# The first expert begun inside the mixer's program, and the small product's stores waited for by ScalarE

## The chip, the core and the metric

The kernel runs on one core of one Trainium2 chip. The core has five engines with instruction queues of their own: TensorE (PE, with its weight loads PEld), VectorE (DVE), ScalarE (ACT), GpSimd (POOL) and SyncE (SP), and 16 DMA engines that all of them feed. The metric is the device time of one execution in microseconds, given as the median of several runs.

## What is computed

Two transformer blocks over 2048 tokens of width 1024, in float32. The change lies where the first block's mixer ends and its experts begin; the rest, cut here, is combine, a second block with attention and a state-space scan, and an output projection.

```python
h = h + concat([ret, pool]) @ w_out            # mixer, 16 tiles of 128 tokens
hn = rms_norm(h, norm_moe_w)
top_vals, top_idx = lax.top_k(hn @ router_w + router_b, 4)      # 4 of 32 experts
gu = ragged_dot(xs, w_gu, group_sizes) + b_gu[sorted_e]         # xs: rows by expert
act = (up + 1.0) * (gate * sigmoid(1.702 * gate))
y = ragged_dot(act, w_down, group_sizes) + b_down[sorted_e]
...
h = h + gate * (p @ ple_proj_w)                # p @ ple_proj_w is the "small product"
```

## The kernel before

Each phase is a program of its own for the five engines. A phase ends when every engine has reached a barrier; then the engines clear the phase's semaphores, each its share, meet at a second barrier, and begin the next phase. There is no scheduler: the order on each engine is the order in which the code is written, and semaphores written by hand tie the engines together.

**The mixer's end.** After the last of 16 tiles, TensorE works off the small product (`p @ ple_proj_w`, two banks for each tile), ScalarE copies the banks into one of six places of SBUF (`copy_small`, L530), and SyncE stores them to HBM (`store_small`, L389). A copy for tile t waits until the store of tile t - 6 has landed. Beside it VectorE makes the routing tables: `order` (the experts sorted, those with many rows first, L848) and `n_mid`, and GpSimd scatters token numbers into `tok_list`, by expert. At the end SyncE waits for all stores of the small product (L425), since the experts' weights `w_hi` take over that memory.

**The experts.** One loop over 32 experts in the order of `order`. An expert's weights come in 25 units of 512 KB (L1214, SyncE) through five places of a tile `stage`. ScalarE copies a unit to `w_hi` (L1289, "high"), VectorE subtracts that copy from the staged values and writes the rest in bfloat16 to `w_lo` (L1420, "low"), which frees the place for a later unit. Units 0 to 15 are the gate and up weights in four chunks of four units, 16 to 24 the down weights. A tile of rows is gathered by GpSimd: token numbers from `tok_list` (`ids`, L1244), then an indirect load of those rows of `hn` (L1250). TensorE turns the rows (L1635), ScalarE and VectorE split them (L1300, L1302, L1425), and TensorE multiplies them with the four chunks (L1105, L1106 with `w_hi`, L1108 with `w_lo`) into banks `GU`. Chunk 3 uses the bank of chunk 0 again, so it waits until VectorE has added the bias to chunk 0 (L1444); on VectorE that addition stands behind the low part of unit 16.

ScalarE begins the phase with the issue of the five bias loads of the first expert (L1278, L1283), and VectorE with tables of row starts (`tables`, L1516 to L1543), which all engines wait for after the first tile of rows.

Of the kernel before, what the change touches and what calls it, by code (L numbers as in the profile page):

```python
# [142 lines left out]
def mixer_phase(nc, I, S):  # L143
# [3 lines left out]
    with ExitStack() as ctx:  # L147
# [7 lines left out]
        stage = sb("mixer_stage", [P, 5 * 1024])  # L155
# [109 lines left out]
            dve_chain list_zeroed y_zeroed slots_seen totals_ps  # L265
            p_in ple_in ple_high ple_low pT_ps pT_hi_done pT_lo_done pT_bf_done pp_ps pp_sb""".split() + [f"pp_stored{n}" for n in range(PP_SLOTS)]
# [4 lines left out]
        s["scattered"] = S["scattered"]  # L271
        block = ctx.enter_context(nc.Block())
# [10 lines left out]
        def _(sp):  # L283
# [146 lines left out]
        def _(pool):  # L430
# [32 lines left out]
            with pool.Fori(0, TILES) as t:  # L463
                body(t)
        @block.scalar
# [149 lines left out]
        def _(dve):  # L615
# [211 lines left out]
            n_mid, is_long, upto, place, other = (stage[:, 4096 + n * E:4096 + (n + 1) * E] for n in range(5))  # L827
            sel, picked = (stage[:, 2048 + n * E * E:2048 + (n + 1) * E * E].rearrange("p (i e) -> p i e", e=E) for n in range(2))
# [19 lines left out]
            dve.tensor_copy(S["order"][:, :], other)  # L848
            dve.tensor_copy(S["n_mid"][:, :], n_mid)
# [268 lines left out]
def expert_phase(nc, I, S):  # L1118
# [6 lines left out]
    with ExitStack() as ctx:  # L1125
# [6 lines left out]
        stage = S["stage"]  # L1132
# [3 lines left out]
        ids = sb("ids", [P, 1], I32)  # L1136
# [20 lines left out]
            y_stored y_seen dve_chain pool_chain tables_ready tables_seen table_chain low_free""".split()  # L1157
        s = {n: sem(n) for n in names}
        st_in = [sem(f"st_in{b}") for b in range(STAGES)]
        bg_in = [s[f"bg_in{c}"] for c in range(GU_CHUNKS)]  # L1160
        ctx.enter_context(nc.allow_non_contiguous_dma(reason="a tile's token numbers, a word per partition"))
        s.update({f"st_in{b}": x for b, x in enumerate(st_in)})
        ctx.callback(clear_semaphores, nc, dict(s))

        s.update({n: S["keep"].enter_context(nc.semaphore(n)) for n in ("ids_in", "rows_in")})
# [7 lines left out]
        def experts(eng, first, mid, last):  # L1173
# [14 lines left out]
            eng.wait_ge(s["tables_ready"], 1)  # L1188
            eng.sem_inc(s["tables_seen"], 1)
# [19 lines left out]
        def _(sp):  # L1209
# [24 lines left out]
        def _(pool):  # L1234
            ch = Chain(pool, s["pool_chain"])
            make_identity(pool, ch, ident[:, :], s["ident_ready"])
            pool.wait_ge(S["scattered"], 16 * TOPK * TILES)
            pool.sem_inc(s["ids_seen"], 1)

            def gather(slot, g, n):  # L1240


                for h in range(2):
                    pool.dma_start(ids[h * HALF:(h + 1) * HALF, :],  # L1244
                                   S["tok_list"][bass.ds(slot + h * (n - HALF), HALF)]).then_inc(s["ids_in"], 16)
# [14 lines left out]
            def first(i, g):  # L1260
                gather(slot_of(i, 0), g, P)
# [11 lines left out]
        def _(act):  # L1273
# [137 lines left out]
        def _(dve):  # L1411
# [109 lines left out]
            def tables():  # L1521


                part = lambda n: w_lo[:, GU_CHUNKS + n // 2, n % 2 * 4:n % 2 * 4 + 4, :].bitcast(F32).rearrange("p k (i e) -> p (k i) e", e=E)
                sel, picked = part(0), part(1)
                iota, zero, order, n_mid, sorted_mid, cnt_t, ends_t, cnt, ends = (pre[:, n * E:(n + 1) * E] for n in range(9))
                numbers(iota, zero)
                tc.link(dve.tensor_copy(order, S["order"][:, :]))
                tc.link(dve.tensor_copy(n_mid, S["n_mid"][:, :]))
                tc.link(dve.tensor_tensor(sel, row_of_e(iota), row_of_i(order), ALU.is_equal))  # L1530
                tc.link(dve.tensor_tensor(picked, sel, row_of_e(n_mid), ALU.mult))
                tc.link(dve.tensor_reduce(sorted_mid, picked, AX, ALU.add))
                tc.link(dve.tensor_scalar(sorted_mid[:, 0:1], sorted_mid[:, 0:1], 1.0, None, ALU.max))
                tc.link(dve.tensor_scalar(sorted_mid[:, E - 1:E], sorted_mid[:, E - 1:E], 1.0, None, ALU.max))
                dve.tensor_copy(S["n_mid"][:, :], sorted_mid)
                tc.link(dve.tensor_scalar(cnt_t, sorted_mid, 2.0, None, ALU.add))
                tc.link(dve.tensor_scalar(cnt, sorted_mid, 4.0, None, ALU.add))
                tc.link(dve.tensor_tensor_scan(ends_t, cnt_t, zero, 0.0, ALU.add, ALU.add))
                tc.link(dve.tensor_tensor_scan(ends, cnt, zero, 0.0, ALU.add, ALU.add))
                tc.link(dve.memset(S["starts"][:, 0:1], 0))  # L1540
                tc.link(dve.memset(S["rows64"][:, 0:1], 0))
                tc.link(dve.tensor_copy(S["starts"][:, 1:E + 1], ends_t))
                tc.link(dve.tensor_copy(S["rows64"][:, 1:E + 1], ends))  # L1543
                dve.sem_inc(s["tables_ready"], 1)
# [2121 lines left out]
```

## Time and profile before

| | us |
|---|---|
| median of 3 runs | 5382.48 (5380.03 to 5384.93) |
| the profiled execution | 5380.71 |
| its span, first to last instruction | 5378.6 |
| TensorE busy | 5094.7 |
| VectorE busy | 3268.8 |
| ScalarE busy | 2190.6 |
| GpSimd busy | 628.2 |

Busy time is the union of an engine's instructions. All times in rows are microseconds from the start of the span, unless a row is marked ns. A timeline row gives start, duration, engine, line, operation, tiles and the number of instructions merged, then in brackets how long the engine had been idle and what released it. A row "A <- B: total, times, longest" is a wait of A that B ended. The DMA share is the mean busy share of the 16 DMA engines; values over 1 mean that packets overlapped.

### The profile page before, as it was taken

The numbers are of one execution on the slowest core, as the hardware profiler recorded it, in microseconds if no ns is written. First come the engines' busy times: TensorE is split into PE (matmuls) and PEld (weight loads), VectorE is DVE, ScalarE is ACT, GpSimd is POOL, SyncE is SP. The second block draws the span as 40 slices with busy tenths as digits, with TensorE's granted clock in tenths as the row PEclk, the third lists the DMA queues.
The fourth block names the chain that finished last, engine by engine and source line by source line (L and its number), as shares of the span: only waits on it lengthen the run. The fifth ranks groups of instructions, "written<-read, shape, count | busy, mean of one in ns | idle before, by whom it ended". The sixth has DMA issues, their size and how long they took to land. (4 is left out here: it accounts for less than half of the span.)

```text
span 5378.6 us, 78209 instructions
## 1 busy us (share of the span) xinstructions
PE 5094.7 (95%) x25188; PEld 3499.3 (65%) x25566; DVE 3268.8 (61%) x6237; ACT 2190.6 (41%) x3309; POOL 628.2 (12%) x862
## 2 busy tenths in 40 slices
PE   7999999799999999999999999979998899999698
PEld 4666665466666666666666666646665688887365
DVE  5444445577777777777777777754557544443266
ACT  4222222354544445555555555333332533333244
POOL 0000000100000000000000000011100399100000
PEclk9999999899999999999999999989999999999899
DMA  8777777665655657777777777453332400000533
GB/s 283 236 253 235 247 242 217 198 202 179 188 192 179 201 170 235 233 231 235 238 239 237 241 234 236 153 190 140 130 115 99 126 7 7 7 7 9 192 110 107
DMA packets 437589, 938.21 MB, mean 174 GB/s; under 512 B 61152, under 2 KB 86176, under 8 KB 436640
## 3 DMA queue, kind: packets, MB, share of 16 engines
q1 hardware_dynamic: 374816, 774.40, 44.1%
q10 hardware_dynamic: 35328, 87.57, 5.1%
q0 software_dynamic: 27280, 74.02, 4.3%
q8 instruction: 106, 1.74, 0.1%
q14 instruction: 59, 0.48, 0.0%
HBM read 781.97 MB, written 155.98 MB: 174 GB/s over the span
## 5 line engine op out<-in xcount | busy, mean ns | idle before, releaser
L1420 DVE TENSOR_TENSOR w_lo_gate<-stage,w_hi 128x1024 bf16<-128x1024 f32 (+1 forms) x800 | 929.8, 1179 | 188.9 <-ACT w_hi L1289 132.0
L1289 ACT ACTIVATE w_hi<-stage 128x1024 fp32r<-128x1024 f32 (+1 forms) x800 | 791.4, 1017 | 557.0 <-PE GU L1108 299.3
L1105 PE MATMUL GU<-w_hi,x_hl 128*128 128x512 f32 x2048 | 860.8, 420 | 16.5 <-DVE x_hl L1425 10.5
L1106 PE MATMUL GU<-w_hi,x_hl 128*128 128x512 f32 x2048 | 811.7, 396 | 0.0
L1108 PE MATMUL GU<-w_lo_gate,x_bf 128*128 128x512 bf16 x1920 | 479.8, 380 | 7.7
L1105 PEld LDWEIGHTS GU<-w_hi,x_hl 128*128 128x128 f32 x2048 | 387.0, 189 | 132.3 <-issue 32.9
L1105 PE MATMUL Y<-w_hi,a_hl 128*128 128x512 f32 x1024 | 456.7, 446 | 1.7 <-DVE a_hl L1431 1.7
L1106 PEld LDWEIGHTS GU<-w_hi,x_hl 128*128 128x128 f32 x2048 | 388.0, 189 | 83.0
L1106 PE MATMUL Y<-w_hi,a_hl 128*128 128x512 f32 x1024 | 404.4, 395 | 0.0
L1108 PEld LDWEIGHTS GU<-w_lo_gate,x_bf 128*128 128x128 bf16 x2048 | 174.4, 98 | 254.5 <-issue 88.4
L2915 DVE TENSOR_REDUCE ntop<-SC 128x1 f32<-128x2048 f32 x64 | 146.7, 2292 | 268.0 <-PE SC L3028 268.0
L1295 ACT ACTIVATE acted<-pre 128x256 f32<-128x256 f32 (+1 forms) x304 | 132.0, 434 | 383.2 <-DVE pre L1448 373.9
L1250 POOL DMA_INDIRECT rows<-hn,ids x77 | 79.9, 1038 | 1737.0 <-PE TX L1635 1698.8
L1108 PE MATMUL Y<-w_lo_gate,a_bf 128*128 128x512 bf16 x960 | 273.3, 383 | 4.4
L3053 PE MATMUL O<-w_lo_gate 128*128 128x128 f32 x2048 | 265.0, 275 | 0.2 <-ACT w_lo_gate L2846 0.2
L1444 DVE TENSOR_TENSOR pre<-GU,b_gu 128x512 f32<-128x512 f32 x256 | 175.8, 687 | 130.0 <-PE GU L1108 129.4
L3053 PEld LDWEIGHTS O<-w_lo_gate 128*128 128x128 f32 x2048 | 246.2, 191 | 1.8 <-ACT w_lo_gate L2846 0.5
L902 PE MATMUL TR<-mixer_stage,c_all 128*128 128x512 f32 x512 | 230.6, 601 | 17.1 <-DMA mixer_stage<-w_out_rows 15.4
L2243 PE MATMUL G<-w_lo_gate,hT 128*128 128x512 f32 x512 | 227.2, 598 | 3.7 <-ACT hT L1922 3.7
L1105 PE MATMUL Z<-w_in_hi,x_hi 128*128 128x512 f32 (+1 forms) x512 | 214.8, 420 | 13.7 <-DVE x_lo L2030 11.5
L1105 PEld LDWEIGHTS Y<-w_hi,a_hl 128*128 128x128 f32 x1024 | 193.2, 189 | 53.1 <-DVE a_hl L1431 2.1
L1106 PEld LDWEIGHTS Y<-w_hi,a_hl 128*128 128x128 f32 x1024 | 193.9, 189 | 33.8
(635 smaller groups left out, 9178.4 us busy)
## 6 DMA issues: line engine op xcount, KB each, us to landing
stage<-in_expert_w_gate_up_dram SPq DMA_DIRECT2D x512, 512.0 KB, 5.2
stage<-in_expert_w_down_dram SPq DMA_DIRECT2D x224, 512.0 KB, 5.5
mixer_stage<-w_in_lo SPq DMA_DIRECT2D x150, 512.0 KB
mixer_stage<-in_w_out_dram SPq DMA_DIRECT2D x65, 512.0 KB, 9.3
expert_rows<-zero_y SPq DMA_DIRECT2D x64, 512.0 KB
mixer_stage<-w_out_rows SPq DMA_DIRECT2D x64, 512.0 KB
b_gu<-in_expert_b_gate_up_dram ACTq DMA_DIRECT2D x128, 256.0 KB, 4.8
expert_rows<-acted ACTq DMA_DIRECT2D x64, 512.0 KB, 3.3
```

Of the source, the lines that this page charges most:

```text
L902: mm = pe.matmul(out, catT[:, k, :], rows[:, q, :], start=(part == 0 and pair == 0 and q == 0), stop=(part == 1 and pair == 1 and q == 1))
L1105: pe.matmul(out, high(k), w_high(k), start=(k == first), stop=False)
L1106: pe.matmul(out, low(k), w_high(k), start=False, stop=False)
L1108: mm = pe.matmul(out, short(k), w_low(k), start=False, stop=(k == last))
L1250: pool.indirect_dma_start(rows[:, :], None, S["hn"], bass.IndirectOffsetOnAxis(ap=ids[:, :], axis=0)).then_inc(s["rows_in"], 16)
L1289: act.activation(w_hi[:, c, ks, :], staged, ACT.Copy).then_inc(s["hi_done"], 1)
L1295: act.activation(act_of(c)[0:n], gate[0:n], ACT.Tanh, scale=ALPHA / 2).then_inc(s["tanh_ready"], 1)
L1420: dve.tensor_tensor(w_lo[:, c, ks, :], staged, w_hi[:, c, ks, :], ALU.subtract).then_inc(s["lo_done"], 1)
L1444: ch.link(dve.tensor_tensor(pre[:, :], GU[c][:, :], b_gu[:, cols], ALU.add))
L2243: mm = pe.matmul(G[:, n * BANK:(n + 1) * BANK], hT[:, k, :], w_gate[:, k, n * BANK:(n + 1) * BANK], start=(k == 0), stop=(k == KD - 1))
L2915: dve.tensor_reduce(ntop[:, h % 2:h % 2 + 1], SC[:, :], AX, ALU.min).then_inc(s["max_done"], 1)
L3053: mm = pe.matmul(O[:, h * P:(h + 1) * P], c_rows(kt), probsT[:, j, kt % 4 * P:(kt % 4 + 1) * P], start=(kt == 0), stop=(kt == TILES - 1))
```

## The change

Five loads of weights, the load of the first token numbers and the work on tables go from the experts' program to the end of the mixer's; the wait for the small product's stores goes from SyncE at the mixer's end to ScalarE at the experts' beginning.

```diff
@@ mixer, SyncE
-            for t in range(3, TILES):
+            for t in range(3, 9):
                 store_small(t)
-            for n in range(PP_SLOTS):
-                sp.wait_ge(s[f"pp_stored{n}"], 16 * len(range(n, TILES, PP_SLOTS)))
+            sp.wait_ge(s["order_ready"], 1)
+            e = sp.value_load(S["order"][0:1, bass.ds(0, 1)], min_val=0, max_val=E - 1)
+            for m, (c, k0, k1) in enumerate(UNITS[0:STAGES]):
+                w = I["expert_w_gate_up"][0, bass.ds(e, 1), k0 * P:k1 * P, c * BANK:(c + 1) * BANK].squeeze(0)
+                sp.dma_start(S["stage"][:, m, 0:k1 - k0, :], w.rearrange("(k p) n -> p k n", p=P)).then_inc(S["st_in"][m], 16)
+            for t in range(9, TILES):
+                store_small(t)
@@ mixer, GpSimd
+            pool.wait_ge(s["scattered"], 16 * TOPK * TILES)
+            pool.wait_ge(s["order_ready"], 1)
...
+            for h in range(2):
+                pool.dma_start(S["ids"][h * HALF:(h + 1) * HALF, :],
+                               S["tok_list"][bass.ds(slot + h * HALF, HALF)]).then_inc(S["ids_in"], 16)
@@ mixer, VectorE
-            dve.tensor_copy(S["order"][:, :], other)
-            dve.tensor_copy(S["n_mid"][:, :], n_mid)
+            dve.tensor_copy(S["order"][:, :], other).then_inc(s["order_ready"], 1)
+            sorted_mid = is_long
+            ch.link(dve.tensor_tensor(picked, sel, row_of_e(n_mid), ALU.mult))
+            ch.link(dve.tensor_reduce(sorted_mid, picked, AX, ALU.add))
...
@@ experts, all engines
             first(0, 0)
-            eng.wait_ge(s["tables_ready"], 1)
-            eng.sem_inc(s["tables_seen"], 1)
@@ experts, SyncE
-            for m in range(N_UNITS):
-                if m >= STAGES:
-                    sp.wait_ge(s["lo_done"], m - STAGES + 1)
+            for m in range(STAGES, N_UNITS):
+                sp.wait_ge(s["lo_done"], m - STAGES + 1)
                 load(m, e)
@@ experts, ScalarE
-            for c in range(GU_CHUNKS):
+            for n in range(PP_SLOTS):
+                act.wait_ge(s[f"pp_stored{n}"], 16 * len(range(n, TILES, PP_SLOTS)))
+            for m in range(4):
+                high(0, m)
+            bias(0, 0)
+            x_high(0)
+            for c in range(1, GU_CHUNKS):
+                high(0, c + 3)
                 bias(0, c)
+            high(0, 7)
             bias_down(0)
-            for m in range(STAGES):
-                high(0, m)
-            x_high(0)
-            for m in range(STAGES, 16):
+            for m in range(8, 16):
                 high(0, m)
@@ experts, VectorE
-            tables()
-            for m in range(STAGES):
+            for m in range(4):
                 low(0, m)
             x_low(0)
-            for m in range(STAGES, 14):
+            for m in range(4, 14):
                 low(0, m)
```

For this `stage`, its semaphores and `ids` are made before the mixer and live through the whole kernel. The mixer's own staging tile lies on `stage`, and so do tiles of attention (`probs`, `cos`, `sin`), of the scan's output (`toep`, `yT`) and of the last projection (`x2`, `gain_post`, `y_in`, `a_in`), which had memory of their own; VectorE's first tables lie on `c_all` and `vgu`.

SyncE at the end of the mixer, before: `pp` is the small product in HBM, `w_in_room` its place in SBUF, and the branch at L147 is the way to the barrier.

```order
L389 DMA pp<-w_in_room 256x1x512 [waits pp_sb] x13
L147 UNCONDITIONAL_BRANCH [waits pp_stored5,pp_stored4,h_stored,pp_stored3,hn_stored,pp_stored2,y_zeroed,pp_stored1,pp_stored0]
L70 UNCONDITIONAL_BRANCH [waits barrier_Pool_Activation_PE_DVE_SP_release]
L73 ISA x19
L69 UNCONDITIONAL_BRANCH
L1208 UNCONDITIONAL_BRANCH [waits barrier_Pool_Activation_PE_DVE_SP_release]
L1171 TENSOR_LOAD order
L1171 ISA x2
L1214 ISA
L1214 DMA stage<-in_expert_w_gate_up_dram 128x2x512
```

The same place on SyncE, with the change:

```order
L390 DMA pp<-w_in_room 256x1x512 [waits pp_sb] x6
L425 TENSOR_LOAD order [waits order_ready]
L425 ISA x2
L428 ISA
L428 DMA stage<-in_expert_w_gate_up_dram 128x2x512
...
L428 DMA stage<-in_expert_w_gate_up_dram 128x2x512
L390 DMA pp<-w_in_room 256x1x512 [waits pp_sb] x7
L147 UNCONDITIONAL_BRANCH [waits y_zeroed,hn_stored,h_stored]
```

The five loads now stand between the sixth and the seventh of those thirteen stores, and the barrier is reached without a wait for the stores.

ScalarE from the beginning of the experts' program, before: `TX` holds the turned rows.

```order
L1283 DMA b_d<-in_expert_b_down_dram 128x1024
L1289 ACTIVATE w_hi<-stage 128x1024 [waits st_in0]
L1289 ACTIVATE w_hi<-stage 128x1024 [waits st_in1]
L1289 ACTIVATE w_hi<-stage 128x1024 [waits st_in2]
L1289 ACTIVATE w_hi<-stage 128x1024 [waits st_in3]
L1289 ACTIVATE w_hi<-stage 128x1024 [waits st_in4]
L1300 ACTIVATE x_hl<-TX 128x8x128 [waits xT_ps]
```

The same place on ScalarE, with the change:

```order
L1311 ACTIVATE w_hi<-stage 128x1024 [waits pp_stored4,pp_stored3,pp_stored5,pp_stored2,st_in0,pp_stored1,pp_stored0]
L1311 ACTIVATE w_hi<-stage 128x1024 [waits st_in1]
L1311 ACTIVATE w_hi<-stage 128x1024 [waits st_in2]
L1311 ACTIVATE w_hi<-stage 128x1024 [waits st_in3]
L1199 TENSOR_LOAD order
L1199 ISA x2
L1300 ISA
L1300 DMA b_gu<-in_expert_b_gate_up_dram 128x512
L1322 ACTIVATE x_hl<-TX 128x8x128 [waits xT_ps]
```

The first copy now carries the wait for the stores, one unit fewer stands ahead of the rows, and the bias loads come after the first four copies, the last four of them behind the rows.

## Rows read from the trace of the kernel before

**Rows 1.** The page's first part: each engine's busy time, share, instructions.

```profile
PE 5094.7 (95%) x25188; PEld 3499.3 (65%) x25566; DVE 3268.8 (61%) x6237; ACT 2190.6 (41%) x3309; POOL 628.2 (12%) x862
```

**Rows 2.** Stretches: from:to, length, busy of PE, PEld, DVE, ACT, POOL; PEclk, DMA, GB/s.

```profile
955.00:965.00 10.00, 9.93 (x44) 6.41 (x45) 2.96 (x5) 4.33 (x8) 1.08 (x1) 1.00 1.01 123
965.00:975.00 10.00, 9.93 (x45) 6.35 (x44) 0.00 (x0) 4.51 (x8) 0.00 (x0) 1.00 0.65 248
975.00:985.00 10.00, 3.56 (x16) 1.85 (x14) 0.00 (x0) 1.92 (x4) 0.00 (x0) 0.78 0.41 156
...
995.00:1005.00 10.00, 0.06 (x1) 0.09 (x2) 5.73 (x5) 4.23 (x4) 1.76 (x1) 0.50 1.04 390
...
1015.00:1025.00 10.00, 9.93 (x45) 6.68 (x45) 5.63 (x5) 5.17 (x5) 1.07 (x2) 1.00 0.97 340
...
1060.00:1200.00 140.00, 136.49 (x656) 89.40 (x664) 103.97 (x169) 65.18 (x96) 9.40 (x14) 1.00 0.54 171
```

**Rows 3.** Timeline of TensorE from the mixer's last product to chunk 3.

```profile
977.95 0.60 PE L1108 MATMUL PJ<-w_in_room 128*128 128x512 bf16 x2
1004.94 1.94 PE L1635 MATMUL TX<-ident,rows 128*128 128x128 f32 x8 [26.39 <-DMA rows<-hn,ids]
1009.30 0.77 PE L1105 MATMUL GU<-w_hi,x_hl 128*128 128x512 f32 x1 [2.42 <-issue]
...
1026.55 1.90 PE L1108 MATMUL GU<-w_lo_gate,x_bf 128*128 128x512 bf16 x7
1032.04 0.76 PE L1105 MATMUL GU<-w_hi,x_hl 128*128 128x512 f32 x1 [3.60 <-DVEq L1450]
```

**Rows 4.** SyncE around the barrier: timeline, its wait, its semaphore at the barrier.

```profile
979.22 0.53 SPq L389 DMA_DIRECT2D pp<-w_in_room  x1
...
986.71 3.22 SPq L1214 DMA_DIRECT2D stage<-in_expert_w_gate_up_dram  x5
...
SPq L425 <- DMA pp<-w_in_room: 2.8, 1, 2.8
...
L69 SPq EVENT_SEMAPHORE  x1: 17/17/17, 985.6 to 985.6; - x1
```

**Rows 5.** Timeline of GpSimd at the beginning of the experts.

```profile
988.26 1.15 POOL L1244 DMA_DIRECT2D ids<-tok_list  x2 [1.89 <-issue]
996.53 1.76 POOL L1250 DMA_INDIRECT rows<-hn,ids  x1 [7.12 <-DMA ids<-tok_list]
...
1011.46 1.80 POOL L1250 DMA_INDIRECT rows<-hn,ids  x1 [2.61 <-DMA ids<-tok_list]
```

**Rows 6.** The gathered rows from 985 to 1300: duration ns (least/median/most), landing.

```profile
L1250 POOL DMA_INDIRECT rows<-hn,ids x11: 1011/1017/1798, 996.5 to 1293.4; - x11
...
DMA to landing us min/median/max: 4.2/4.7/8.3
```

**Rows 7.** Timeline of ScalarE: small product's copy, bias issues, weight copies.

```profile
977.28 0.60 ACT L530 ACTIVATE w_in_room<-PJ 128x512 f32<-128x512 f32 x1 [0.83 <-PE PJ L1108]
...
986.70 3.72 ACTq L1278 DMA_DIRECT2D b_gu<-in_expert_b_gate_up_dram  x4
...
1008.93 4.83 ACT L1289 ACTIVATE w_hi<-stage 128x1024 fp32r<-128x1024 f32 x5
...
1028.39 1.06 ACT L1289 ACTIVATE w_hi<-stage 128x1024 fp32r<-128x1024 f32 x1 [1.94 <-DMA stage<-in_expert_w_down_dram]
```

**Rows 8.** Timeline of VectorE: order, first split, first bias addition.

```profile
957.80 0.18 DVE L848 CAST order<-mixer_stage 128x32 int32<-128x32 f32 x1
...
994.65 1.23 DVE L1420 TENSOR_TENSOR w_lo_gate<-stage,w_hi 128x1024 bf16<-128x1024 f32 x1 [1.65 <-ACT w_hi L1289]
...
1030.62 0.68 DVE L1444 TENSOR_TENSOR pre<-GU,b_gu 128x512 f32<-128x512 f32 x1
```

**Rows 9.** The store of small tile 9: its issue and landing.

```profile
L389 SPq DMA_DIRECT2D pp<-w_in_room x1: 533/533/533, 962.7 to 962.7; - x1
...
DMA to landing us min/median/max: 5.6/5.6/5.6
```

More of the change, by code:

```diff
@@ L464, in _ @@
                 body(t)
+            pool.wait_ge(s["scattered"], 16 * TOPK * TILES)
+            pool.wait_ge(s["order_ready"], 1)
+            pool.sem_inc(s["lists_seen"], 1)
+            e = pool.value_load(S["order"][0:1, bass.ds(0, 1)], min_val=0, max_val=E - 1)
+            slot = nc.s_assert_within(pool.snap(e * CAP), 0, E * CAP - P,
+                                      skip_runtime_bounds_check_because="an expert has CAP places in the list")
+            for h in range(2):
+                pool.dma_start(S["ids"][h * HALF:(h + 1) * HALF, :],
+                               S["tok_list"][bass.ds(slot + h * HALF, HALF)]).then_inc(S["ids_in"], 16)
         @block.scalar
@@ L826, in _ @@
             dve.wait_ge(s["totals_ps"], 1)
-            n_mid, is_long, upto, place, other = (stage[:, 4096 + n * E:4096 + (n + 1) * E] for n in range(5))
-            sel, picked = (stage[:, 2048 + n * E * E:2048 + (n + 1) * E * E].rearrange("p (i e) -> p i e", e=E) for n in range(2))
+            n_mid, is_long, upto, place, other = (c_all[:, n * E:(n + 1) * E] for n in range(5))
+            sel, picked = (vgu[:, n, 0:E * E].rearrange("p (i e) -> p i e", e=E) for n in range(2))
             row_of_e = lambda ap: ap.unsqueeze(1).to_broadcast([P, E, E])
@@ L847, in _ @@
             ch.link(dve.tensor_reduce(other, picked, AX, ALU.add))
-            dve.tensor_copy(S["order"][:, :], other)
-            dve.tensor_copy(S["n_mid"][:, :], n_mid)
+            dve.tensor_copy(S["order"][:, :], other).then_inc(s["order_ready"], 1)
+            sorted_mid = is_long
+            ch.link(dve.tensor_tensor(picked, sel, row_of_e(n_mid), ALU.mult))
+            ch.link(dve.tensor_reduce(sorted_mid, picked, AX, ALU.add))
+            ch.link(dve.tensor_scalar(sorted_mid[:, 0:1], sorted_mid[:, 0:1], 1.0, None, ALU.max))
+            ch.link(dve.tensor_scalar(sorted_mid[:, E - 1:E], sorted_mid[:, E - 1:E], 1.0, None, ALU.max))
+            dve.tensor_copy(S["n_mid"][:, :], sorted_mid)
+            dve.memset(S["starts"][:, 0:1], 0)
+            dve.memset(S["rows64"][:, 0:1], 0)
+            for table, ends, more in (("starts", upto, 2.0), ("rows64", place, 4.0)):
+                ch.link(dve.tensor_scalar(other, sorted_mid, more, None, ALU.add))
+                ch.link(dve.tensor_tensor_scan(ends, other, zero_e[:, :], 0.0, ALU.add, ALU.add))
+                dve.tensor_copy(S[table][:, 1:E + 1], ends)
         @block.tensor
@@ L3604, in two_blocks @@
             "n_long": sb("n_long", [P, 1], I32),
+            "stage": sb("stage", [P, STAGES, KP, BANK], F32),
+            "st_in": [ctx.enter_context(nc.semaphore(f"st_in{b}")) for b in range(STAGES)],
+            "pp_stored": [ctx.enter_context(nc.semaphore(f"pp_stored{n}")) for n in range(PP_SLOTS)],
+            "ids": sb("ids", [P, 1], I32),
+            "ids_in": ctx.enter_context(nc.semaphore("ids_in")),
             "pos_cur": sb("pos_cur", [P, TOPK], I32),
```

76 lines of the change are left out of this document (26 added, 50 removed).

## The prediction

> **What bounds the kernel now.** I read the page's busy times first [rows 1]: TensorE is busy 95% of the span, so only stretches in which it stands still or waits can give time back. The table of stretches finds the place [rows 2]. In the experts' loop TensorE works 136.49 of 140 us (1060 to 1200). Between the last small product of the mixer, at 977.95, and the first weight product of the first expert, at 1009.30, it only turns one tile of rows [rows 3], and between 995 and 1005 its granted clock is 0.50, the lower of its two levels (1.2 of 2.4 GHz). That hole is 31 us, and a smaller one follows: chunk 2 is issued out about 1028.5, and chunk 3 starts at 1032.04 after 3.6 us of waiting for VectorE [rows 3].
>
> The waits say what ends the hole. SyncE issues the last store of the small product at 979.22 and waits 2.8 us until it has landed; the barrier behind the clearing of semaphores opens at 985.6 [rows 4]. GpSimd then issues the load of the token numbers at 988.26 and stands 7.1 us until they are in, starts the gather of rows at 996.53, and that lands 8.3 us later, the slowest of eleven (4.2, 4.7 and 8.3 are least, median and most) [rows 5, 6]. TensorE turns the rows at 1004.94 and its idle time ends on that gather [rows 3]. While the gather was under way the DMA engines were full: share 1.04 and 390 GB/s [rows 2], with ten units of weights and five bias loads. So the chain is stores, barrier, numbers, gather, turn, and the weights are beside it.
>
> **The change, part by part.** All is reckoned against the profiled execution, span 5378.6 and time 5380.71 us; the median of the three runs is 5382.48, 1.77 more, and I take a difference over from one to the other.
>
> 1. The wait for the stores leaves SyncE. Of its 2.8 us I leave 0.3 for the three waits that stay (h, hn, zeroed rows, all issued long before). The barrier then opens at 985.6 - 2.5 = 983.1. The six waits now stand in ScalarE ahead of its first weight copy; behind them are all its copies, and VectorE and TensorE behind those. The last store lands about 982.6 as before (979.75 + 2.8), ahead of the new start, so I cost them at nothing; the cover is the gather, below, and holds until the landing is some 3 us later.
>
> 2. The numbers are loaded in the mixer. GpSimd's gather takes the place of the load at 988.26, 2.6 us after the barrier, with one of two table reads gone: 2.1 us. New start 983.1 + 2.1 = 985.2 instead of 996.53.
>
> 3. The gather's landing. Bounds are 4.2 and 8.3 us [rows 6]. Five units are in the stage by then, so the queue it met at 996 is gone, but from about 986 SyncE loads units 5 to 8 as VectorE frees places, and VectorE works beside it: the first two gathers took GpSimd 1.76 and 1.80 us against a median of 1.02 [rows 5, 6]. I take the middle, 6.4: rows in at 991.6, turned from 991.7, against 1004.94: 13.2 us earlier (2.5 barrier, 8.8 numbers, 1.9 landing). The weights are ready: four copies of 0.97 us from 983.5 (five in 4.83 us [rows 7]) with VectorE's 1.23 us each behind them [rows 8] end at 989.4. From the turn to the first product is 4.36 us [rows 3], the same instructions in the same order: first product at 996.1 instead of 1009.30.
>
> 4. From there to chunk 3. Before, this took 22.7 us (1009.30 to 1032.04). Chunk 3 needs VectorE's first bias addition, at 1030.62, which stands behind the splitting of unit 16, which ScalarE copied at 1028.39 [rows 7, 8]. Before, five units were split and five staged when the product began; now four are split and five staged, so the refill is one unit behind: 0.52 MB at 390 GB/s, 1.3 us. Four bias loads (3 x 0.26 and 0.52 MB, 3.4 us at that rate) come in here, which were issued at 986.70 before [rows 7]. ScalarE issues them between copies, 0.93 us each (four in 3.72), beside a copy of 0.97. They start while the stage is full and DMA has little to do, and in the ten microseconds from 1015 on DMA moved 340 GB/s [rows 2], not all it can. Bounds: 3.6 us less (the wait ahead of chunk 3 gone, TensorE's three chunks back to back) and 4.7 more (unit and biases in full). I take 1.2 more, near the unit alone. Chunk 3 at 996.1 + 23.9 = 1020.0, that is 12.0 us earlier. After it the order is the old one and the loop is bound by TensorE [rows 2], so the 12.0 us are carried to the end.
>
> 5. The table work on VectorE moves into the mixer. There it runs beside the small products, after the copy of the order at 957.80; VectorE did nothing at all from 965 to 985 [rows 2, 8]. At its old place it cost nothing either: VectorE's first split waited 1.65 us for ScalarE [rows 8]. Moved for free, and the barrier pair that it needed goes too.
>
> 6. Five loads ahead of stores 9 to 15 on SyncE. The order is ready at 958.0 [rows 8]. Stores go out every 2.75 us (store 9 at 962.7, store 15 at 979.22 [rows 4, 9]), so store 8 leaves at about 960; the table read and five issues take some 4 us (five issues in 3.22 [rows 4]), and store 9 waits until about 965. Its data stand behind 2.62 MB, 6.7 us at 390 GB/s: landed at 968.3 before (5.6 us after issue [rows 9]), now about 975. ScalarE needs that landing for its copy at 977.28 [rows 7], the only copy whose place was stored after the loads: 2.3 us to spare. Room for the bytes: DMA's share is 0.65 and 0.41 from 965 to 985 [rows 2], 9.4 us free of 20 against 6.7. Cost: nothing.
>
> The Trainium skill speaks against point 6: its page "DMA: Bandwidth & Descriptors", section "Queues, rings and completion order", says that each DMA engine consumes the descriptors of one queue in ring order. By that, stores cannot pass the loads; no row of before shows it, as no such loads stand there.
>
> 7. The other edits move buffers (the stage now lives through the kernel, tiles of attention and output lie on it). Their instructions and waits stay; I cost them at zero, within 1 us either way.
>
> Sum: 5380.71 - 12.0 = 5368.7 for the profiled execution, 5370.5 on the median's scale. With points 3 and 4 at their ends the gain is 6.6 to 19 us.
>
> **The rivals.**
> *The refill takes it back.* Unit 16 is late by the unit and all bias bytes, 4.7 us instead of 1.2: gain 8.5, or 6.6 with the slowest gather. For it: 390 GB/s for ten microseconds [rows 2]. Against it: the loads start 11 us earlier. 5374.0.
>
> *The gather starts after the splits.* In the new order the gather runs beside VectorE's first four splits, which lasted 1.23 us each. If GpSimd cannot write before they end at 989.4 and the rows land a median 4.7 us later, they come at 994.1, 2.5 us after my 991.6: gain 9.5, 5373.0. Against it: the two gathers beside splits took 0.75 us more, not the length of several splits [rows 5, 6].
>
> The Trainium skill, page "SBUF — State Buffer", section "SBUF: two separate sides", states this rule: a VectorE instruction with two inputs in SBUF and GpSimd share a pair of ports that one holds for a whole instruction while the other is blocked. The 1.76 and 1.80 us bear it out only as far as part of one split. By the rule the gain is 9.5 us, by those two rows 12.0.
>
> *It doesn't do what it says.* If unit 16 comes no earlier than 1028.4, only the barrier's 2.5 us are left, 5380.0. From 986.7 to then 12 units, the biases and two gathers are 8.9 MB: DMA would have to fall to 213 GB/s, where rows show 340 and 390 under load [rows 2].
>
> *Slower: the stores crawl behind the loads.* From 955 to 965 DMA moved 123 GB/s at a share of 1.01 [rows 2]. From 961 on, stores 7 to 15 and the loads are 7.3 MB. At 123 GB/s the last store lands at 1020; ScalarE, now holding the wait, copies four units after that (3.9 us), issues a bias (0.9) and makes the two copies of the rows (some 3 with VectorE's part), so the first product is about 8 us behind, 1028 instead of 1009: with the refill 20 us slower, 5402. It decides against the kernel where the last landing is after some 1000, a mean below 187 GB/s. Against it: 248 GB/s from 965 to 975 with stores alone [rows 2], which went at ScalarE's pace.
>
> **How the numbers follow.** A measurement of this kernel tells about 0.2% from no change, here 10.8 us. Forecast, a gain of 9.5 to 15.5 (5367 to 5373): 0.62. More, with chunk 3 straight behind chunk 2: 0.04. Refill 0.15, splits 0.10, no effect 0.05, slower 0.04. The line of 10.8 us cuts the forecast: four fifths of it, 0.50, are above, with 0.04 and 0.02 of the splits' case that is 0.56 for faster; 0.40 for the same; 0.04 for slower. The range takes gains of 6 to 16 us, 5366.5 to 5376.5, and leaves out the last two cases and the edges, under 0.2.
>
> **What would show it.** In the trace of after: the barrier opening near 983 and no wait of SyncE for the last store; the gather starting near 985 and landing 5 to 8 us later; the rows turned near 992, first product near 996, chunk 3 near 1020, and the same distance from there to the end. ScalarE's copy of small tile 15 still near 977. The forecast is wrong if the small products end later than 980, if ScalarE's first copy is after 988, if the gather lands after 994, or if the loop from 1060 on takes other times than before.

## The result, and the profile after

The kernel after takes 5351.26 us (median of six runs, 5342.78 to 5364.98), the kernel before 5382.3 beside it: a ratio of 0.994, with a 95% interval from 0.9928 to 0.9953. The forecast was 5370.5 with a range from 5366.5 to 5376.5. The gain is 31 us where 12 were forecast, and the time lies below the range. The profiled execution of after took 5342.78 us, its span is 5341.0, 37.6 less than that of before.

The hole at the experts' beginning closed much as forecast. Timelines of after, TensorE first (start, duration, engine, line, operation, tiles, number; in brackets the idle time and what ended it), then SyncE, GpSimd, ScalarE and VectorE:

```profile
986.62 1.94 PE L1636 MATMUL TX<-ident,rows 128*128 128x128 f32 x8 [10.69 <-DMA rows<-hn,ids]
990.98 0.77 PE L1132 MATMUL GU<-w_hi,x_hl 128*128 128x512 f32 x1 [2.42 <-issue]
1007.75 0.58 PE L1132 MATMUL GU<-w_hi,x_hl 128*128 128x512 f32 x1 [4.12 <-DVE w_lo_gate L1447]
1016.39 0.47 PE L1132 MATMUL GU<-w_hi,x_hl 128*128 128x512 f32 x1 [1.38 <-DVEq L1477]
...
959.44 3.01 SPq L428 DMA_DIRECT2D stage<-in_expert_w_gate_up_dram  x5
...
964.96 1.15 POOL L478 DMA_DIRECT2D ids<-tok_list  x2 [11.49 <-issue]
...
982.00 1.05 POOL L1272 DMA_INDIRECT rows<-hn,ids  x1 [1.20 <-issue]
...
974.65 0.60 ACT L546 ACTIVATE w_in_room<-PJ 128x512 f32<-128x512 f32 x1 [0.83 <-PE PJ L1135]
...
982.10 2.00 ACT L1311 ACTIVATE w_hi<-stage 128x1024 fp32r<-128x1024 f32 x2 [5.54 <-DMA pp<-w_in_room]
...
983.19 4.63 DVE L1447 TENSOR_TENSOR w_lo_gate<-stage,w_hi 128x1024 bf16<-128x1024 f32 x4 [23.71 <-ACT w_hi L1311]
```

The gathered rows of after from 980 to 1300, to be set beside [rows 6] (duration in ns, then landing in us, least, median and most):

```profile
L1272 POOL DMA_INDIRECT rows<-hn,ids x11: 1011/1014/1261, 982.0 to 1276.9; - x11
...
DMA to landing us min/median/max: 4.2/4.5/8.9
```

The rows are turned at 986.62 instead of 1004.94 and the first product comes at 990.98 instead of 1009.30 [rows 3]. The numbers are loaded at 964.96 in the mixer, the gather starts at 982.00 instead of 996.53 [rows 5], and ScalarE's first weight copy now waits until the last store has landed (`<-DMA pp`). Chunk 2 has a new wait of 4.12 us, chunk 3's fell from 3.60 to 1.38.

But that is not where most of the gain is. The experts' loop from the first mid tile's first product to the first turned rows of the phase behind it, two rows of before and then the same two of after:

```profile
1055.79 0.52 PE L1657 MATMUL GU<-w_hi,x_hl 128*128 128x512 f32 x1
...
3532.89 0.45 PE L2226 MATMUL TR<-ident,h 128*128 128x128 f32 x1 [29.34 <-DVEq L2044]
```

```profile
1040.86 0.50 PE L1658 MATMUL GU<-w_hi,x_hl 128*128 128x512 f32 x1
...
3498.17 0.45 PE L2227 MATMUL TR<-ident,h 128*128 128x128 f32 x1 [29.28 <-DVEq L2045]
```

After is 14.93 us ahead at the loop's beginning and 34.72 at its end: 2477.10 us became 2457.31 in a stretch whose program the change hardly touches. No wait went away there: from 1080 to 3400 TensorE's longest is 0.9 us in both, and the granted clock from 1100 to 3400 is 1.00, the upper level of 2.4 GHz, in both. From turning to turning, 62 full tiles of 128 rows take 34.31 us each instead of 34.61, one as the other, and the twelve mid tiles of 64 rows 21.95 instead of 22.01 (medians). The gain sits in one kind of product. Groups of TensorE from 2100 to 2900, before and then after (busy time and mean ns of one; the ends are modelled, so a mean holds time that a product waits in the engine, and some bfloat16 records of before are missing):

```profile
L1106 PE MATMUL GU<-w_hi,x_hl 128*128 128x512 f32 x744 | 293.8, 395 | 0.0
L1108 PE MATMUL GU<-w_lo_gate,x_bf 128*128 128x512 bf16 x694 | 173.5, 380 | 2.8
```

```profile
L1133 PE MATMUL GU<-w_hi,x_hl 128*128 128x512 f32 x744 | 290.6, 391 | 0.0
L1135 PE MATMUL GU<-w_lo_gate,x_bf 128*128 128x512 bf16 x743 | 180.5, 381 | 0.0
```

The float32r products are 4 ns shorter, the bfloat16 ones the same. The pitch, from the start of one float32r weight load to the start of the next load, went from 231.8 to 228.4 ns in the mean for the gate and up products, and from 231.4 to 229.8 for the down products.

The rest of the pair's 37.6 us: 2.6 at the mixer's end (its last small product starts at 975.55 instead of 978.18), and 3 behind the loop. In the thirteen traces of this document the mixer ends anywhere from 970.2 to 983.8, with either program, so the 2.6 us can't be put down to the change. What the 3 us come from stays open. Distances below are therefore counted from the mixer's end, "+15.4" being 15.4 us behind the start of its last small product.

### The profile page after: what moved, and what is told of

The parts are those of the page before. It is cut to its first block and busy times, and to the rows that moved or that the text cites. A ratio compares the mean times of both kernels' runs of the same rounds, so it can differ in the third digit from the quotient of the medians.

```text
span 5341.0 us, 78576 instructions
## 1 busy us (share of the span) xinstructions
PE 5098.8 (95%) x25565; PEld 3497.4 (65%) x25566; DVE 3261.3 (61%) x6229; ACT 2191.0 (41%) x3309; POOL 626.5 (12%) x862
## 5 line engine op out<-in xcount | busy, mean ns | idle before, releaser
L1132 PE MATMUL GU<-w_hi,x_hl 128*128 128x512 f32 x2048 | 851.5, 416 | 18.4 <-DVE x_hl L1452 10.5
L1133 PE MATMUL GU<-w_hi,x_hl 128*128 128x512 f32 x2048 | 802.8, 392 | 0.0
L1135 PE MATMUL GU<-w_lo_gate,x_bf 128*128 128x512 bf16 x2048 | 498.4, 381 | 0.0
L1135 PE MATMUL Y<-w_lo_gate,a_bf 128*128 128x512 bf16 x1024 | 287.8, 383 | 0.0
L929 PE MATMUL TR<-stage,c_all 128*128 128x512 f32 x512 | 231.6, 603 | 15.6 <-DMA stage<-w_out_rows 13.0
```

The costliest lines, as they stand in the source:

```text
L929: mm = pe.matmul(out, catT[:, k, :], rows[:, q, :], start=(part == 0 and pair == 0 and q == 0), stop=(part == 1 and pair == 1 and q == 1))
L1132: pe.matmul(out, high(k), w_high(k), start=(k == first), stop=False)
L1133: pe.matmul(out, low(k), w_high(k), start=False, stop=False)
L1135: mm = pe.matmul(out, short(k), w_low(k), start=False, stop=(k == last))
```

## The experiments

### Does the place of `w_hi` set the tile time?

The change moves almost every buffer. `w_hi` went from byte 87328 of its partition to 87360; the first is 32 over a multiple of 64, the second is one. `x_hl`, the split rows that TensorE loads as weights, stayed at 202560. In these four kernels only unused bytes are laid between buffers (`after_again` changes nothing).

```diff
@@ before_w64: kernel before; after_w32: kernel after
+        sb("pad_w", [P, 8])
         w_hi = sb("w_hi", [P, CHUNKS_W, KD, BANK], F32R)
...
+        sb("pad_r", [P, 8])
         rows = sb("rows", [P, D])
@@ after_x32: kernel after
+        sb("pad_r", [P, 8])
         rows = sb("rows", [P, D])
```

> The kernel before, with 32 bytes left free per partition ahead of w_hi, and 32 more ahead of rows: w_hi moves from byte 87328 to 87360, the place it has in the kernel after (a multiple of 64, which 87328 is not); x_hl moves by 64 bytes and keeps its remainder. Nothing of the program changes. Theory P (place: the products that read w_hi run faster because w_hi now starts at a multiple of 64): a full tile of the experts' loop takes 34.31 us instead of 34.61, and the time falls by the 20 us that the loop gained, to about 5362. Theory O (the loop is faster because of the order or the state in which the program enters it, not because of the place): 34.61 us a tile, 5382. Theory V (it varies from run to run): either.

> The kernel after, with 32 bytes left free ahead of w_hi and 32 ahead of rows: w_hi goes from byte 87360 to 87392, off the multiple of 64 again as in the kernel before; x_hl keeps its remainder. Theory P: a full tile takes 34.61 us again, the time rises by about 20 us to 5370 (what the program's change alone is worth, 12 us below the kernel before). Theory O: 34.31 us, 5350.

> The kernel after, with 32 bytes left free ahead of rows alone: w_hi stays at a multiple of 64, and x_hl, x_bf and a_hl, which TensorE loads as weights, move off it. Theory P in its narrow form (what is streamed counts, the 512 columns of w_hi): no change, 34.31 us a tile, 5350. In its wide form (any operand of TensorE counts): the tiles get slower, by up to 0.3 us each, up to 5370.

> The kernel after, unchanged, beside the others on one chip. Theories P and O: 34.31 us a tile in its profile and 5343 to 5355. Theory V (a tile's time varies from run to run by the 0.3 us): a tile time other than 34.31, or times that spread over the 20 us that the six runs so far did.

Measured, ratios to the kernel before on the same chip: `before_w64` 1.0009 (0.9999 to 1.0019), `after_w32` 0.9967 (0.9953 to 0.9982), `after_x32` 0.9973 (0.9964 to 0.9983), `after_again` 0.9943 (0.9926 to 0.9959).

`after_again` repeats 34.31 us, so theory V falls. `before_w64` falsifies theory P: `w_hi` is where the kernel after has it and the tiles take 34.67 us, more than before. In `after_x32` `w_hi` did not move and the tiles are back at 34.61. What orders all of them is the distance from `w_hi` to `x_hl`:

| kernel | w_hi | x_hl | distance | full tile, us | loop, us |
|---|---|---|---|---|---|
| before | 87328 | 202560 | 115232 | 34.61 | 2477.1 |
| after_w32 | 87392 | 202624 | 115232 | 34.61 | 2477.4 |
| after_x32 | 87360 | 202592 | 115232 | 34.61 | 2476.4 |
| before_w64 | 87360 | 202624 | 115264 | 34.67 | 2480.9 |
| after, after_again | 87360 | 202560 | 115200 | 34.31 | 2457.3, 2458.5 |

Three different placements with one distance have one tile time. The place of `w_hi` doesn't count, the distance does: theory D.

### Is it the distance, and in TensorE alone?

`before_d0` gives the kernel before the distance of after by laying 32 bytes ahead of `w_hi` and allocating `ids` last; `after_both` moves both operands of after by 32 bytes. `micro_d` is no version of the kernel: it runs 16 float32r products at a time, one source line for each distance, with `w_hi` at one place and `x_hl` read from further on.

```diff
@@ before_d0: kernel before
+        sb("pad_w", [P, 8])
         w_hi = sb("w_hi", [P, CHUNKS_W, KD, BANK], F32R)
...
-        ids = sb("ids", [P, 1], I32)
         rows = sb("rows", [P, D])
...
+        ids = sb("ids", [P, 1], I32)
@@ after_both: kernel after
+        sb("pad_w", [P, 8])
         w_hi = sb("w_hi", [P, CHUNKS_W, KD, BANK], F32R)
```

> The kernel before, unchanged, beside the others on one chip, for its tiles and its mixer there. Its x_hl begins 115232 bytes behind w_hi. Theory D (the distance from w_hi, which TensorE streams, to x_hl, which it loads as the next weights meanwhile, sets the pitch of the float32r products): a full tile takes 34.61 us, as in the profile of before and in the two changed kernels that have the same distance. Theory V (it varies from load to load): another tile time.

> The kernel before, with 32 bytes free ahead of w_hi and the gather's numbers (ids) allocated last instead of ahead of rows: w_hi moves from byte 87328 to 87360, x_hl stays at 202560, so the distance falls from 115232 to the 115200 of the kernel after; the program is untouched. Theory D: a full tile takes 34.31 us and the time falls by the loop's 20 us, to about 0.9963 of before. Theory O (the loop is faster because of how the program enters it): 34.61 us, no change of time.

> The kernel after, with 32 bytes free ahead of w_hi: w_hi and x_hl both move by 32, to bytes 87392 and 202592, neither a multiple of 64; the distance stays 115200. Theory D: 34.31 us a full tile, the time of the kernel after (5345 beside it on the last chip). Theory P in its wide form (both operands have to start at a multiple of 64 bytes): 34.61 us or more, 20 us longer.

> Nothing of the kernel but its float32r products: 16 products (eight k, high and low half) of one chunk, with w_hi 115200 bytes ahead of x_hl as in the kernel after, then the same 16 with x_hl read 32, 64, ... 480 bytes further on, and 4, 16, 48, 512, 1024 and 2048, one source line each, twice over, without DMA, VectorE or ScalarE beside them; the output is zeros. Theory D: the pitch differs from line to line, lowest at +0 (some 227 ns) and higher at +32 (some 232) and +64 (some 233), and the curve shows whether another distance is better. If the lines do not differ, the distance acts through another engine's accesses (VectorE and ScalarE write x_hl and w_hi) and not in TensorE alone.

`before_again` took 0.9996 of before (0.9986 to 1.0005), with 34.61 us a tile. `before_d0` took 0.9965 (0.9953 to 0.9978), that is 19 us less, with 34.31 us a tile and the program of before. Its loop, from the same two rows:

```profile
1057.85 0.50 PE L1658 MATMUL GU<-w_hi,x_hl 128*128 128x512 f32 x1
...
3515.78 0.45 PE L2227 MATMUL TR<-ident,h 128*128 128x128 f32 x1 [29.24 <-DVEq L2045]
```

These are 2457.93 us. `after_both`, with both operands off a multiple of 64, kept 34.31 us and 0.9939 (0.9922 to 0.9955). So theory D stands and theories O and P fall: 32 bytes are worth 19 to 20 us, with no instruction changed.

The timeline of TensorE in `micro_d`, 16 products a row; L57 has distance 115200, each further line up to L72 32 bytes more, L65 256 more; L73 to L78 are +4, +16, +48, +512, +1024 and +2048, and L79 is +0 again:

```profile
38.89 3.80 PE L57 MATMUL G<-w_hi,x_hl 128*128 128x512 f32 x16
42.52 3.89 PE L58 MATMUL G<-w_hi,x_hl 128*128 128x512 f32 x16
46.25 3.90 PE L59 MATMUL G<-w_hi,x_hl 128*128 128x512 f32 x16
49.98 3.90 PE L60 MATMUL G<-w_hi,x_hl 128*128 128x512 f32 x16
53.72 3.88 PE L61 MATMUL G<-w_hi,x_hl 128*128 128x512 f32 x16
57.44 3.90 PE L62 MATMUL G<-w_hi,x_hl 128*128 128x512 f32 x16
61.17 3.84 PE L63 MATMUL G<-w_hi,x_hl 128*128 128x512 f32 x16
64.85 3.89 PE L64 MATMUL G<-w_hi,x_hl 128*128 128x512 f32 x16
68.58 3.80 PE L65 MATMUL G<-w_hi,x_hl 128*128 128x512 f32 x16
72.21 3.89 PE L66 MATMUL G<-w_hi,x_hl 128*128 128x512 f32 x16
75.94 3.90 PE L67 MATMUL G<-w_hi,x_hl 128*128 128x512 f32 x16
79.67 3.90 PE L68 MATMUL G<-w_hi,x_hl 128*128 128x512 f32 x16
83.41 3.88 PE L69 MATMUL G<-w_hi,x_hl 128*128 128x512 f32 x16
87.13 3.90 PE L70 MATMUL G<-w_hi,x_hl 128*128 128x512 f32 x16
90.86 3.84 PE L71 MATMUL G<-w_hi,x_hl 128*128 128x512 f32 x16
94.54 3.90 PE L72 MATMUL G<-w_hi,x_hl 128*128 128x512 f32 x16
98.27 3.88 PE L73 MATMUL G<-w_hi,x_hl 128*128 128x512 f32 x16
101.99 3.80 PE L74 MATMUL G<-w_hi,x_hl 128*128 128x512 f32 x16
105.62 3.89 PE L75 MATMUL G<-w_hi,x_hl 128*128 128x512 f32 x16
109.35 3.79 PE L76 MATMUL G<-w_hi,x_hl 128*128 128x512 f32 x16
112.98 3.79 PE L77 MATMUL G<-w_hi,x_hl 128*128 128x512 f32 x16
116.60 3.79 PE L78 MATMUL G<-w_hi,x_hl 128*128 128x512 f32 x16
120.23 3.80 PE L79 MATMUL G<-w_hi,x_hl 128*128 128x512 f32 x16
```

The difference of two starts over 16 is the pitch. At +0 (L57) it is 3.63 / 16 = 226.9 ns; at +32 and +64 3.73 / 16 = 233.1; at +192 (L63) 3.68 / 16 = 230; at +256 (L65) 226.9 again, and at +288 233.1 again. So the curve has a period of 256 bytes, and the distance that the change fell into by its new allocations, 115200 = 450 x 256, is as good as any measured. The later lines repeat it: +512, +1024 and +2048 give 226.3 to 226.9, +4 gives 232.5, and +16 is as good as +0. No instruction of VectorE, ScalarE or GpSimd runs beside these products, and of DMA five single packets, so no other engine is needed for the effect. What is left are TensorE's own two reads, the streamed operand and the next weights loaded under it; that is by exclusion, and how the memory or the engine makes them meet was not shown.

In the kernel the good distance pays mainly in long runs. A gate or up chunk is a run of 16 float32r products between bfloat16 ones, the last one broken into two runs of 8. In after, the median pitches within a run of 16, from start to start of the products and without the first, are 224, 231, 236, 228, 232 and 231 ns, and then eight of 227; in before all fourteen lie between 230 and 235. In the runs of 8 the mean without the first fell only from 232.0 to 231.0. The down products have the same good distance (`a_hl` begins 16384 bytes behind `x_hl`) but come in runs of 8 and 4, with means from 233.5 to 232.0 and from 232.4 to 232.0. Why it takes some six products stays open.

The Trainium skill, page "SBUF — State Buffer", section "Who interferes with whom", lists two independent read ports for TensorE, one for the moving operand and one for weight loads, and lets only the port pair of VectorE and GpSimd cause contention. The 233.1 against 226.9 ns differ with nothing but the distance of those two reads; for float32r operands the measurement decides, and the time of a product is not independent of where the two reads lie.

### Do the other phases gain by it too?

`after_align` brings the mixer's, the states' and the output phase's float32r operands to distances of multiples of 256.

```diff
+        sb("pad_mx", [P, 40])
         x_hi, x_lo, x_bf = (sb(n, [P, KD, P], dt) for n, dt in (("mx_hi", F32R), ("mx_lo", F32R), ("mx_bf", BF16)))
+        sb("pad_x2", [P, 32])
         x2_hi = sb("x2_hi", [P, KD, P], F32R)
+        sb("pad_g", [P, 56])
         g_hi, g_lo, g_bf = (sb(n, [P, KS, P], t) for n, t in (("g_hi", F32R), ("g_lo", F32R), ("g_bf", BF16)))
+        sb("pad_c", [P, 40])
         c_hi, c_lo, c_bf = (sb(n, [P, KD, P], t) for n, t in (("c_hi", F32R), ("c_lo", F32R), ("c_bf", BF16)))
```

> The kernel after, with bytes left free so that in the other three phases with float32r products, too, the distance from what is streamed to what is loaded as the next weights is a multiple of 256: mx_hi moves 160 bytes from w_in_hi in the mixer (distance 96 over a multiple of 256 before), x2_hi 128 from w_in2_hi in the states' phase (128 over), g_hi 224 and c_hi 128 from w_6_hi in the output phase (32 and 128 over). The program and the experts' tiles stay. Theory D in full (any float32r product runs by that curve: 226.7 ns at a multiple of 256 against 230 to 233.5): the mean pitch falls by some 4 to 6 ns in about 1200 back-to-back products of the mixer, 960 of the states' phase and 600 of the output phase, and as TensorE is busy 96 to 98% in all three, the kernel gets 8 to 15 us shorter than after, to about 0.991 to 0.992 of before. If those phases' pitch hangs on something else (they hold two separate tiles of halves instead of one interleaved tile), no change.

Measured: 5341.43 us, 0.9925 of before (0.9908 to 0.9942), the lowest ratio of all, but its interval overlaps with those of the unchanged kernel after (0.9928 to 0.9953). The pitch fell by less than forecast: 228.9 and 231.4 ns for the mixer's high and low halves (230.7 and 233.4 in after), 228.0 and 229.3 in the output product (230.7 and 233.6). From the states' first turned rows to their last product of Z it is 609.67 us against 612 to 614.3 in the nine traces before it, so 2 to 5 us are gained there in this one trace. From the end of the experts' loop to the end of the kernel it takes 1837.1 us, against 1841.5 to 1846.8 in the twelve other traces. The mixer ended at 983.35, no earlier than the 981.1 to 983.8 of the three kernels below on the same chip. A gain of the 8 to 15 us is not shown; that the distance counts for other products, too, is, with a smaller size. Whether their runs are too short, as those of the down products, was not tested.

### What the program's own change was worth

Three kernels, each the kernel after with one part undone, each run once; what follows is read from their traces.

```diff
@@ after_spwait: SyncE, mixer's end (and the same loop taken out of ScalarE)
+            for n in range(PP_SLOTS):
+                sp.wait_ge(s[f"pp_stored{n}"], 16 * len(range(n, TILES, PP_SLOTS)))
             sp.wait_ge(s["h_stored"], 16 * TILES)
@@ after_ids: GpSimd, mixer's end
-            for h in range(2):
-                pool.dma_start(S["ids"][h * HALF:(h + 1) * HALF, :],
-                               S["tok_list"][bass.ds(slot + h * HALF, HALF)]).then_inc(S["ids_in"], 16)
@@ after_ids: GpSimd, experts
-                gather(None if is_step(i, 0) else slot_of(i, 0), g, P)
+                gather(slot_of(i, 0), g, P)
@@ after_order: ScalarE (VectorE likewise with STAGES for 4)
+            for c in range(GU_CHUNKS):
+                bias(0, c)
+            bias_down(0)
+            for m in range(STAGES):
+                high(0, m)
+            x_high(0)
```

> The kernel after with one part undone: SyncE waits for the small product's stores at the mixer's end again and ScalarE does not. By the forecast's first step the barrier opens 2.5 us later against the mixer's last small product (980.05 less 975.55 in after, so +4.5, becomes +7), the gather starts as much later, and ScalarE's 1.7 us in its own wait go: the first product, +15.4 in after, comes at about +18. Rival: the last store lands at +6.3 whoever waits, so that only the time from there to the gather counts, and the first product comes at +17.

> The kernel after with one part undone: the first gather's numbers are loaded in the experts' program, not in the mixer's. They took 5 to 6 us from issue to landing there. By the forecast's second step the gather starts at about +13 behind the mixer's last small product instead of +6.5, and the first product comes at +21.5 to +22 instead of +15.4; the mid tile's first product, +65.3 in after, at about +71. Rival: the loads go slower with the stage's refill beside them, as in the kernel before, where the gather started 11 us behind the barrier: +15 and +24.

> The kernel after with one part undone: ScalarE issues the five bias loads first and both engines copy and split five pieces ahead of x_high and x_low, as in the kernel before. The issues take ScalarE 4.4 us (5 at 0.9 to 1.2), and its first copy of a weight piece starts that much later, at some +11 against +6.5; the rows are turned at +12.6 by then, so ScalarE's copy of x comes behind five pieces, at about +16 instead of +13, and the first product at +18.5 instead of +15.4. The forecast held the other side: pieces freed earlier, and chunk 3 of the first tile (+40.8 in after) earlier by up to the 2.7 us that the refill cost. Rival: the bias loads take nothing from the copies, since they are issued by ScalarE's queue while it has to wait for the stores anyway (1.7 us), and +17.

Counted from the mixer's end; "mid" is the first product of the second tile, where what was won in the first is in hand. Landing is the gather's, from its start; "split" is VectorE's first split, from the gather's start.

| kernel | barrier | gather starts | split | landing | first product | mid |
|---|---|---|---|---|---|---|
| before | +7.46 | +18.36 | -1.88 | 8.27 | +31.12 | +77.61 |
| before_again | +7.46 | +18.67 | -2.01 | 8.35 | +31.51 | +77.15 |
| before_d0 | +7.46 | +18.47 | -1.73 | 8.65 | +31.62 | +77.31 |
| before_w64 | +7.46 | +18.53 | -2.03 | 7.59 | +30.61 | +77.40 |
| after | +4.50 | +6.44 | +1.20 | 4.49 | +15.43 | +65.31 |
| after_both | +4.51 | +6.45 | +1.87 | 4.45 | +15.39 | +63.98 |
| after_align | +4.50 | +6.45 | +1.20 | 4.46 | +15.41 | +64.92 |
| after_w32 | +4.50 | +6.44 | +0.87 | 5.32 | +16.25 | +65.10 |
| after_again | +4.54 | +6.48 | +0.35 | 5.99 | +16.96 | +66.59 |
| after_x32 | +4.50 | +6.44 | -0.05 | 7.70 | +18.63 | +66.94 |
| after_spwait | +8.50 | +10.44 | -0.70 | 7.18 | +22.12 | +70.95 |
| after_ids | +4.50 | +11.74 | -4.16 | 7.77 | +24.00 | +73.44 |
| after_order | +4.50 | +6.45 | +7.26 | 4.34 | +20.71 | +67.94 |

The four traces with the old program have the mid tile at +77.4 in the mean, the six with the whole new one at +65.5: the program's change is worth 11.9 us. The times agree as far as they go: `after_w32` and `after_x32`, the new program at the old distance, take 0.9967 and 0.9973 of before, 18 and 15 us less, with intervals from 10 to 25 and from 9 to 19.

`after_spwait` fits neither number: the barrier opens at +8.50, not +7, since the last store lands later than in before (4.6 us after its issue, against 3.4) and the barrier follows 2.9 us behind the landing, and the first product comes at +22.1. Moving the wait is worth 5.5 us to the mid tile. `after_ids` starts its gather at +11.74, earlier than forecast, as its two loads land 2.2 and 3.3 us after their issues here (6.3 and 6.8 in before), but the gather lands as slowly as the rival had it: +24.0, and 8 us to the mid tile. `after_order` makes ScalarE's first copy wait for five bias issues (+12.62 instead of +6.55), with the first product at +20.7 and 2.5 us lost at the mid tile. The old order does help the refill, 23.53 us from the first product to chunk 3 instead of 25.41, but not enough: chunk 3 comes at +44.24 instead of +40.84. The three sum to more than the 11.9; that each one undone changes what the others hide would explain it, but pairs of them were not run.

The table shows what goes with a gather that lands sooner. Where VectorE's first split comes 1.2 us or more behind the gather's start, it lands after 4.3 to 4.5 us; where the split comes within the first microsecond, after 5.3 to 6.0; where it has begun before, after 7.2 to 8.65. GpSimd and VectorE in `after_x32`, where the gather starts 0.06 us behind the splits, and in `after_order`, where VectorE begins its splits 7 us behind:

```profile
981.41 2.10 POOL L1273 DMA_INDIRECT rows<-hn,ids  x1 [1.20 <-issue]
...
981.35 4.63 DVE L1448 TENSOR_TENSOR w_lo_gate<-stage,w_hi 128x1024 bf16<-128x1024 f32 x4 [22.35 <-ACT w_hi L1312]
```

```profile
990.25 1.05 POOL L1272 DMA_INDIRECT rows<-hn,ids  x1 [1.21 <-issue]
...
997.51 1.22 DVE L1444 TENSOR_TENSOR w_lo_gate<-stage,w_hi 128x1024 bf16<-128x1024 f32 x1 [29.79 <-ACT w_hi L1311]
```

GpSimd's own instruction takes 2.10 us beside the splits here, 1.39 to 2.06 in the six other traces in which they are under way, and 1.05 in the six in which it starts first. That is not the whole of it: in `after_w32` and `after_again` the instruction takes 1.05 us, too, and the rows still land after 5.3 and 6.0. What splits bring with them can be two things, VectorE itself and the weight loads that SyncE issues for every place they free; no run tells these apart. The Trainium skill's page "SBUF — State Buffer", section "SBUF: two separate sides", says that VectorE and GpSimd share a pair of ports that one of them holds for a whole instruction, and that an instruction of VectorE with two inputs in SBUF blocks GpSimd only where GpSimd reads SBUF (the gather reads `ids`). The 1.05 us that the instruction is longer, beside splits of 1.16 each (four in 4.63), agree with it as far as GpSimd's instruction goes.

## Why the prediction was wrong

The step that failed is point 7: "I cost them at zero, within 1 us either way". The buffers that the edits move were worth 19 to 20 us (`before_d0`, 0.9965), more than all that the program's change won. The operands' distance set the pitch of the gate and up products, 231.8 ns at 32 bytes over a multiple of 256 and 228.4 at the multiple. No row of before shows a price for an address, but none excluded one either, so "within 1 us" was not a bound. The forecast's own mark, "if the loop from 1060 on takes other times than before", is what told it. On the median's scale, 5382.3 - 11.9 - 19.2 = 5351.2, against 5351.26 measured; the last term is the loop of `before_again` less that of `before_d0` (2477.08 and 2457.93). That this comes within 0.1 us is luck: it leaves out the 3 us behind the loop, and the mixer's end moves by 13.6 us from trace to trace.

Point by point, from the mixer's end:

1. The barrier: forecast 2.5 us earlier, measured 2.96 (+7.46 to +4.50). The last store lands at +6.31 in after, 1.8 us behind the barrier, against +4.44 in before, so ScalarE's first copy waits for it; I had put this at nothing, with the last landing "as before". The cover that I named held: the gather landed at +10.93. By the table the wait may even have helped, since it keeps the splits behind the gather's start.
2. The numbers: forecast 2.1 us from barrier to gather, measured 1.94.
3. The landing: forecast 6.4 between bounds of 4.2 and 8.3, measured 4.49, and 4.45 to 7.70 in the six traces of the new program. The first product is 15.7 us earlier by the pair, 13.2 forecast.
4. The refill: forecast 1.2 us, measured 25.41 less 22.74, so 2.7, with a wait of 4.12 us ahead of chunk 2 that no step had. Points 3 and 4 missed in opposite directions. In the pair chunk 3 is 13.0 us earlier and the mid tile 12.3, and between the means of the traces it is 11.9; that this lies so near the 12.0 forecast is luck.
5. The table work: no wait shows for it in after.
6. The loads ahead of the stores: ScalarE's copy of small tile 15 starts at 974.65 instead of 977.28 [rows 7], 2.63 us earlier, exactly as the mixer's end; nothing waited. Store 9 landed 11.7 us after its issue, against 5.6 [rows 9], at 974.2, where I had said 975. The row:

```profile
L390 SPq DMA_DIRECT2D pp<-w_in_room x1: 847/847/847, 962.5 to 962.5; - x1
...
DMA to landing us min/median/max: 11.7/11.7/11.7
```

It is 1.3 us behind the last of the five loads (972.9), and the other six land one by one behind it, 1.2 to 1.4 us apart, the last at 981.9. The Trainium skill's page "DMA: Bandwidth & Descriptors", section "Queues, rings and completion order", says that each DMA engine consumes the descriptors of one queue in ring order; these landings agree with it. Point 6 had reckoned with the stores behind the loads, so the rule does not speak against it. What it missed is that all seven stores stay late, so that point 1's last landing is not "as before".

The rivals. "The refill takes it back" had the right mechanism and part of the size, 2.7 of 4.7 us. "The gather starts after the splits" did not happen in after, because the wait for the stores held the splits back. In `after_x32` the gather did start beside them, landed 3.2 us later than in after, and the mid tile is 1.6 us later; but GpSimd's instruction ended at 983.51, before the last split at 985.98, so it did not wait for all of them. "It doesn't do what it says" and "the stores crawl" did not occur: DMA moved 392 GB/s from 965 to 975, where the stores crawling behind loads had been reckoned at 123, and the last landing was at 981.9. The stretch in after, as in [rows 2]:

```profile
965.00:975.00 10.00, 10.00 (x45) 6.42 (x44) 0.00 (x0) 4.52 (x8) 1.10 (x2) 1.00 1.05 392
```

## What to carry to other kernels

A change that moves buffers is two changes: time the move alone, with bytes laid in ahead of the old kernel's buffers, before the gain is put down to the program. Where float32r products run back to back, 16 and more at a time, lay the streamed operand and the weights a multiple of 256 bytes apart; against 32 bytes more that is 2.7% of each product in `micro_d`, 1.5% of the gate and up products in the kernel and 19 us of its time. Start a gather ahead of VectorE's splits and of the loads that they set off, not beside them.

## What the hardware showed that was not expected

- The pitch of back-to-back float32r products (512 columns, weights of 128 columns) hangs on the distance of the two operands in SBUF, with a period of 256 bytes: 226.9 ns at 0 and 16, 230 at 192, 232.5 to 233.8 at 4, 32 to 160 and 224. Moving both operands together by 32 or 64 bytes made no difference. Behind bfloat16 products the good distance settles at 227 ns after some six products; in runs of 8 it gained 1 to 1.5 ns, in runs of 4 only 0.4.
- A gather of 128 rows lands after 4.3 us when VectorE's splits begin 7 us behind its start, and after 7.2 to 8.7 us when they are under way.
